# Memory and forget-gate attention heads laid as steps into the neighbouring projection chunks of a two-block transformer kernel

## The chip, the cores and the metric

The kernel runs on one core of one Trainium2 chip, as one launch. The metric is the device time of that launch in microseconds (us). Engines by their names in the profile: PE is TensorE (matmuls; PEld its weight loads), DVE is VectorE, ACT is ScalarE, POOL is GpSimd, SP is SyncE, which issues the weight transfers.

## The reference, cut to what matters

Two transformer blocks run one after the other over 256 tokens of width 1024, all in float32. The change touches only the second block, whose two layers mix tokens like this (`mk`, `mv`, `k_sh`, `v_sh` and the forget sums are computed earlier):

```
# layer 0
proj = h @ a_w_in                       # 1024 -> 3*1024 + 512
gate_b, gate_c, u, qm = split(proj)     # qm: 4 heads of 128
y_tok = gate_b * causal_depthwise_conv(gate_c * u, a_conv_w)
y_mem = softmax(qm . mk * 128**-0.5) . mv          # 4 "memory" heads
x = x + concat([y_tok, y_mem]) @ a_w_out           # 1536 -> 1024
# layer 1
q, qm = split(h @ b_w_q)                # 8 heads of 128, 4 heads of 128
y_tok = forgetting_attention(q, k_sh, v_sh, c_sh)  # 8 causal "fox" heads
y_mem = softmax(qm . mk1 * 128**-0.5) . mv1        # 4 memory heads
x = x + concat([y_tok, y_mem]) @ b_w_out           # 1536 -> 1024
```

Every head has 256 queries and 256 keys; a fox head is causal, so its first 128 queries see 128 keys.

## The kernel before, in words

**Chunks.** All weights come from memory in chunks of 1 MB (128 partitions by 2048 numbers), two buffers deep. SP loads chunk g into `W_raw` once the split of chunk g-2 is through. ACT rounds it to `W_hi` (L1012), DVE makes the rest `W_lo = W_raw - W_hi` (L1275), and PE multiplies with both parts. This split of chunk g+1 (`ahead`) is the first thing that ACT and DVE do in the body of chunk g.

**Projection chunks** (`up`, `conv`) give 256 output columns each. PE (`up_chunk`, L650 to L656) runs 16 pairs of matmuls into two of the PSUM banks 0 to 3, alternating between two pairs of banks. After the last one ACT copies one half out (`cross`, L1025), DVE adds the other (`add_halves`, L1291), DVE scales by the row factor (`by_rows`, L1300) and raises `acc_read`. **Output chunks** (`down`) take 256 rows of the weight each: 24 matmuls (`down_chunk`, L661 to L663) accumulate over all chunks into banks 4 to 7. Their input, a block of 512 columns of the stage before, is staged first: ACT rounds it (`stage_hi`, L1079, raises `st_hi`), POOL subtracts (L1809, raises `st_lo`), and `down_chunk` begins with `pe.wait_ge(st_lo, staged)`.

**The order of the work** is a list of stages written out in `make_plan`. Each engine walks the whole list in this order and runs its part of each stage; an engine never goes on to a later stage before it has issued all of its part of the earlier one. In layer 0 the list is: `conv` (12 chunks: for each group c of 4, one chunk each of gate_b, gate_c and u), `mem_q` (2 chunks), `attend memory0` (4 heads), `a_out` (6 chunks: 4 blocks of conv output, 2 of heads). In layer 1 it is `fox_q` (4 chunks), `mem_q` (2), `attend fox` (12 heads, two fox and one memory in turn), `b_out` (6).

**The convolution on POOL.** For each group c POOL waits for `acc_read` of its third chunk, multiplies gate_c by u (L1861), then makes three taps: six products (L1868), two sums (L1872), and the product with gate_b (L1873), which raises `conv_done`. Each waits for the one before.

**A head.** PE `scores` (L768), DVE `soft` (row maximum; for fox with the bias, L1338), ACT `exps` (L1086), DVE `normalise` (L1346, L1349), PE `transposes` (L786), ACT `keep_pt` (L1096), PE `values` (L803), DVE `output` (L1361). The first two or three heads' scores stand inside the last `mem_q` chunk (`open_attention`); all the rest is a block of its own, at whose start PE waits for `acc_read` of the last chunk. Scores use banks 4 to 6, transposes banks 0 and 1, values banks 2 and 3.

Of the kernel before, what the change touches and what calls it, by code (L numbers as in the profile page):

```python
# [116 lines left out]
def make_plan(w):  # L117
# [58 lines left out]
    for l in range(2):  # L176
# [30 lines left out]
def build_program(nc, a, out):  # L207
# [19 lines left out]
    with ctx:  # L227
# [163 lines left out]
        for st in stages:  # L391
            st["h0"] = h_count
            if st["kind"] == "attend":
# [7 lines left out]
                for what, h in st["what"]:  # L401
# [4 lines left out]
                    e["paired"] = st["paired"]  # L406
# [37 lines left out]
        for n, e in enumerate(heads):  # L444
# [4 lines left out]
                                (4 + 2 * (u % 2) + i,) if e["paired"] else (4 + n % 3,))  # L449
# [3 lines left out]
            e["pt_banks"] = [0, 1] if e["G"] == 3 else [i if e["paired"] else n % 2]  # L453
# [12 lines left out]
            elif e["paired"]:  # L466
                e["probs"] = region(at + (2 * (u % 2) + i) * width, width)
                e["ptile"] = [region(e["R"]["pt"] + (2 * (u % 2) + i) * 512, 512)]
                e["pt_free"] = u - 1
            else:  # L470
                e["probs"] = region(at + (n % 3) * width, width) if n % 3 < 2 else T1
                e["ptile"] = [region(e["R"]["pt"] + (n % 2) * 512, 512)]
                e["pt_free"] = u - 1
# [10 lines left out]
        k_norm = k_turn = n_glu = n_staged = n_cross = 0  # L484
        for n, st in enumerate(stages):
# [12 lines left out]
            if st["kind"] == "down":  # L498
                st["staged0"] = n_staged
                n_staged += st["n"]  # L500
                before = stages[n - 1]
                before["next_down"] = st
                st["each"] = before["kind"] == "glu" or before.get("dest") == "h"
            if st["kind"] == "attend":
                stages[n - 1]["next_attend"] = st
        before_heads = lambda st: len(stages[stages.index(st) - 1]["what"])

        def e_out_done(n):

            for st in stages:  # L510
                if st["kind"] == "attend" and st["a0"] <= n < st["a0"] + len(st["what"]):
                    return st["h0"] + n - st["a0"] + 1

# [6 lines left out]
        def down_src(st, j):  # L520
# [3 lines left out]
            return U[:, bass.ds(H0 + j * 2 * S, 2 * S)]  # L524


        opened = lambda st: {"even": 2, "dilated": 1, "memory0": 2, "fox": 3}[st["name"]]
# [17 lines left out]
        def _(sp):  # L545
# [9 lines left out]
            for st in stages:  # L555
# [41 lines left out]
                elif kind == "down":  # L597
                    ks = st["ks"]

                    def body(i):  # L600
                        for s in range(2):
                            load(g0 + 2 * i + s, slots[s],
                                 w_[:, bass.ds((2 * i + s) * ks, ks), :], ks, st["ncols"])
                    repeat(sp, n // 2, body)
# [11 lines left out]
        def _(pe):  # L616
# [15 lines left out]
            def up_chunk(g, u, slot, pair, xn=XN, first=True, between=None,  # L632
                         at=(1, 3), by_k=False):
# [66 lines left out]
            def down_chunk(st, g, staged, slot, first, final):  # L700
# [4 lines left out]
                for t in range(TT):  # L705
                    if first and t == 1 and st["src"] == "h" and not st["each"]:
# [4 lines left out]
                    for at, (ks, b) in enumerate(order):  # L711
                        if by_half and t == 0 and ks and not any(k for k, _ in order[:at]):
# [4 lines left out]
                        last = three(PS[:, 4 + 2 * t + b, 0:hi - lo],  # L717
# [73 lines left out]
            def values(u):  # L791

                both = [heads[n] for n in units[u]]
                if u >= 2:
                    pe.wait_ge(h_done, e_out_done(units[u - 2][-1]))
                for e in both:
                    d = (64 if e["paired"] else P)
                    e["o"] = PS[e["pb"]:e["pb"] + d, 2 + u % 2, 0:S]
# [16 lines left out]
                last.then_inc(s_pv, 1)  # L815

# [40 lines left out]
            for st in stages:  # L857
                g0, u0, n, kind = st["g"], st["u"], st["n"], st["kind"]
                slots, pairs = (g0 % 2, (g0 + 1) % 2), (u0 % 2, (u0 + 1) % 2)
                if kind == "norm":  # L860
                    if st["fill"] and not st["again"]:
                        fill_chunk(st, lambda: turn(st))
                    else:
                        if st["x0"] and not st["fill"]:

                            acc_free(u0)
                            for _ in range(3):
                                mm(PS[:, 2 * pairs[0], :], XN[:, 0, 0, 0:P], both_halves(XN, 0),
# [9 lines left out]
                elif kind in ("up", "glu"):  # L878
                    def body(i, ss=(0, 1)):
                        for s in ss:  # L880
# [4 lines left out]
                            if st.get("sums") and starts(i, s - 1):  # L885
# [3 lines left out]
                                     between=between, at=at, by_k=st["led"] and starts(i, s))  # L889
# [4 lines left out]
                elif kind == "conv":  # L894
                    for c in range(n):
                        up_chunk(g0 + c, u0 + c, (g0 + c) % 2, (u0 + c) % 2, first=c == 0,
                                 between=(lambda: spread(st)) if c == 1 else None, at=(1, 0))
# [53 lines left out]
                elif kind == "down":  # L951
                    for j in (0,) if n > 1 else ():
                        down_chunk(st, g0, staged + 1, g0 % 2, True, False)
# [6 lines left out]
                    def body(i):  # L960
                        for s in range(2):
                            down_chunk(st, g0 + 1 + 2 * i + s, staged + 2 + 2 * i + s,
                                       (g0 + 1 + s) % 2, False, False)
                    repeat(pe, mid // 2, body)
# [17 lines left out]
                elif kind == "attend":  # L982
                    a0, m = st["a0"], len(st["what"])

# [3 lines left out]
                    if not st["paired"]:  # L988
                        for u in us[opened(st):3]:
                            scores(u)  # L990
                    for u in us:
# [6 lines left out]
                        if not st["paired"] and u + 3 in us:  # L998
                            scores(u + 3)
# [4 lines left out]
        def _(act):  # L1004
# [76 lines left out]
            def exps(n):  # L1081
                e = heads[n]
                act.wait_ge(s_soft, n + 1)
                for t in range(TT):
# [3 lines left out]
                      accum_out=e["z"][:, t:t + 1]).then_inc(s_exp, 1)  # L1088

# [13 lines left out]
            for st in stages:  # L1103
# [39 lines left out]
                elif kind in ("up", "conv", "natural"):  # L1143
                    def body(i, ss=(0, 1)):
                        for s in ss:
# [9 lines left out]
                            if kind == "up" and s == 1 and st.get("next_attend"):  # L1155
                                exps(st["next_attend"]["a0"])
                            if kind != "natural":
                                cross(g0 + 2 * i + s, u0 + 2 * i + s, pairs[s], st.get("times", 1.0))
                    early = st.get("next_down")
                    loops = n // 2 - bool(early and n > 1)  # L1160
                    if loops and (st["led"] or st["raised"]) and kind != "conv":
# [4 lines left out]
                    else:  # L1166
                        repeat(act, loops, body)
                    if early:
# [46 lines left out]
                elif kind == "down":  # L1215
                    def body(i):
                        for s in range(2):
                            ahead(g0 + 2 * i + s, slots[s])
                            stage_hi(st, 2 * i + s + 2, g0 + 2 * i + s + 2, slots[s])
                    rounds = max(n - 2, 0) // 2  # L1220
                    repeat(act, rounds, body)
# [19 lines left out]
                elif kind == "attend":  # L1241
                    a0, m = st["a0"], len(st["what"])
# [7 lines left out]
                    lead = 2 if st["name"] in ("memory0", "fox", "even") else 1  # L1250
                    for u in st["units"]:
# [5 lines left out]
                        if u == st["units"][-1] - (2 if st["size"] == 1 else 1):  # L1257
# [4 lines left out]
        def _(dve):  # L1262
# [89 lines left out]
            def output(u):  # L1352
# [3 lines left out]
                o = PS[:, 2 + u % 2, 0:S]  # L1356
# [5 lines left out]

            def open_attention(st):


                if st["name"] == "memory0":
                    dve.wait_ge(conv_cu_done, 4)
# [50 lines left out]
            for st in stages:  # L1418
# [48 lines left out]
                elif kind == "up":  # L1467
# [4 lines left out]
                    def body(i, ss=(0, 1)):  # L1472
                        for s in ss:
# [5 lines left out]
                            if s == 1 and st.get("next_attend"):  # L1479
                                open_attention(st["next_attend"])  # L1480
# [126 lines left out]
                elif kind == "conv":  # L1607
                    for c in range(4):
                        for part in range(3):
                            j = 3 * c + part  # L1610
                            if j != 1:
                                ahead(g0 + j, (g0 + j) % 2)
# [6 lines left out]
                            if j == 0:  # L1619
                                ahead(g0 + 1, (g0 + 1) % 2)  # L1620
                                dve.wait_ge(r_kept, rows_at)
                            by_rows(dst, st["sum0"] + j + 1).then_inc(acc_read, 1)
                elif kind == "down":
# [3 lines left out]
                    repeat(dve, (n - 1) // 2, body)  # L1627
# [333 lines left out]
```

## Time and profile before

| | us |
|---|---|
| median of 3 runs (1873.0 to 1874.36) | 1873.25 |
| the profiled execution, its own time | 1875.29 |
| its span | 1873.5 |
| PE busy | 1819.4 (97%) |
| DVE busy | 1211.2 (65%) |
| ACT busy | 936.3 (50%) |
| POOL busy | 299.1 (16%) |
| chain that ended last | PE 91%, DVE 4%, ACT 3% |

Busy is the time in which an engine had an instruction running, over the span. The chain is followed back from the last instruction to whatever released each step. The layer-0 mixing stages run from about 1000 to 1129 us of the span, those of layer 1 from about 1578 to 1679 us.

### The profile page before, as it was taken

The numbers are of one execution on the slowest core, as the hardware profiler recorded it, in microseconds if no ns is written. First come the engines' busy times: TensorE is split into PE (matmuls) and PEld (weight loads), VectorE is DVE, ScalarE is ACT, GpSimd is POOL, SyncE is SP. The second block draws the span as 40 slices with busy tenths as digits, with TensorE's granted clock in tenths as the row PEclk, the third lists the DMA queues.
The fourth block names the chain that finished last, engine by engine and source line by source line (L and its number), as shares of the span: only waits on it lengthen the run. The fifth ranks groups of instructions, "written<-read, shape, count | busy, mean of one in ns | idle before, by whom it ended". The sixth has DMA issues, their size and how long they took to land.

```text
span 1873.5 us, 27530 instructions
## 1 busy us (share of the span) xinstructions
PE 1819.4 (97%) x9737; PEld 1539.3 (82%) x9737; DVE 1211.2 (65%) x1523; ACT 936.3 (50%) x1394; POOL 299.1 (16%) x255
## 2 busy tenths in 40 slices
PE   8899999999999999999999989999999999999998
PEld 6678888888877888888888878888888888778886
DVE  5866755767775665576746756674667656656664
ACT  4455545434456544464545445554554455555553
POOL 1011021211201001210022930002005021020012
PEclk9999999999999999999999999999999999999999
DMA  6326555555521665555555535555555555345553
GB/s 218 130 74 197 180 201 180 180 180 180 180 91 53 195 191 185 195 180 187 193 184 182 186 123 180 193 187 190 182 191 174 185 189 174 108 146 180 188 193 134
DMA packets 215000, 320.29 MB, mean 171 GB/s; under 512 B 6024, under 2 KB 167056, under 8 KB 214672
## 3 DMA queue, kind: packets, MB, share of 16 engines
q1 hardware_dynamic: 213616, 313.45, 50.3%
q0 software_dynamic: 1024, 5.64, 0.8%
q8 instruction: 46, 0.75, 0.2%
q10 hardware_dynamic: 288, 0.23, 0.0%
q14 instruction: 26, 0.21, 0.0%
HBM read 318.24 MB, written 1.06 MB: 170 GB/s over the span
## 4 chain that ended last, share of the span: by engine, by line
PE 91%; DVE 4%; ACT 3%; issue 1%; DMA 1%; DVEq 0%; POOL 0%; POOLq 0%; ACTq 0%; SPq 0%
PE PS L656 26%; PE PS L661 13%; PE PS L663 13%; PE PS L662 13%; PE PS L654 13%; PE PS L650 4%; PE PS L651 2%; PE PS L768 2%; DVE W_lo L1275 2%; PE PS L803 1%; PE PS L786 1%; PE PS L730 1%; ACT U L1096 1%; ACT U L1086 1%; PE PS L919 1%
## 5 line engine op out<-in xcount | busy, mean ns | idle before, releaser
L1275 DVE TENSOR_TENSOR W_lo<-W_raw,W_hi 128x1024 fp32r<-128x1024 f32 x598 | 775.5, 1336 | 292.7 <-ACT W_hi L1012 270.8
L656 PE MATMUL PS<-XN,W_hi 128*128 128x512 f32 x2072 | 740.1, 396 | 0.0
L1012 ACT ACTIVATE W_hi<-W_raw 128x1024 fp32r<-128x1024 f32 x598 | 598.6, 1050 | 176.4 <-PE PS L663 114.5
L654 PE MATMUL PS<-XN,W_lo 128*128 128x256 f32 x2072 | 579.2, 280 | 2.7 <-DVE W_lo L1275 2.7
L656 PEld LDWEIGHTS PS<-XN,W_hi 128*128 128x128 f32 x2072 | 389.6, 188 | 80.2
L654 PEld LDWEIGHTS PS<-XN,W_lo 128*128 128x128 f32 x2072 | 391.4, 189 | 16.6 <-DVE W_lo L1275 3.0
L1809 POOL TENSOR_TENSOR SX<-U,SX 128x512 fp32r<-128x512 f32 (+1 forms) x98 | 128.5, 1315 | 1141.5 <-ACT SX L1079 1141.5
L661 PE MATMUL PS<-W_hi,SX 128*128 128x512 f32 x780 | 303.9, 390 | 1.1 <-DVE W_lo L1275 1.1
L662 PE MATMUL PS<-W_lo,SX 128*128 128x512 f32 x780 | 303.0, 389 | 0.0
L663 PE MATMUL PS<-W_hi,SX 128*128 128x512 f32 x780 | 303.0, 389 | 0.0
L1025 ACT ACTIVATE T<-PS 128x512 f32<-128x512 f32 x152 | 91.0, 599 | 410.5 <-PE PS L656 410.3
L1291 DVE TENSOR_TENSOR T<-PS,T 128x512 f32<-128x512 f32 x128 | 88.4, 691 | 211.3 <-ACT T L1025 211.3
L1079 ACT ACTIVATE SX<-U 128x512 fp32r (+2 forms) x98 | 60.5, 628 | 233.5 <-PE PS L663 230.7
L661 PEld LDWEIGHTS PS<-W_hi,SX 128*128 128x128 f32 x780 | 146.4, 188 | 31.7 <-issue 1.9
L663 PEld LDWEIGHTS PS<-W_hi,SX 128*128 128x128 f32 x780 | 146.4, 188 | 30.4
L662 PEld LDWEIGHTS PS<-W_lo,SX 128*128 128x128 f32 x780 | 146.4, 188 | 30.3
L661 PE MATMUL PS<-W_hi,XN 128*128 128x512 f32 (+1 forms) x352 | 139.1, 395 | 6.0 <-DVE W_lo L1275 3.8
L663 PE MATMUL PS<-W_hi,XN 128*128 128x512 f32 (+1 forms) x352 | 137.3, 390 | 0.0
L662 PE MATMUL PS<-W_lo,XN 128*128 128x512 f32 (+1 forms) x352 | 137.2, 390 | 0.0
L650 PE MATMUL PS<-XN,W_hi 128*128 128x512 f32 x296 | 118.8, 402 | 4.5 <-DVE W_lo L1275 3.3
L661 PEld LDWEIGHTS PS<-W_hi,XN 128*128 128x128 f32 x352 | 66.6, 189 | 20.8 <-DVE W_lo L1275 5.3
L651 PE MATMUL PS<-XN,W_lo 128*128 128x256 f32 x296 | 82.2, 278 | 0.0
(166 smaller groups left out, 1532.1 us busy)
## 6 DMA issues: line engine op xcount, KB each, us to landing
W_raw<-in_ffn_w_gate_up SPq DMA_DIRECT2D x88, 1024.0 KB, 5.0
W_raw<-in_mlp_w SPq DMA_DIRECT2D x64, 1024.0 KB, 5.2
W_raw<-in_ffn_w_down SPq DMA_DIRECT2D x44, 1024.0 KB, 4.8
W_raw<-in_od_w_in SPq DMA_DIRECT2D x36, 1024.0 KB, 5.1
W_raw<-in_a_w_in SPq DMA_DIRECT2D x14, 1024.0 KB, 4.9
W_raw<-in_mem_w_kv SPq DMA_DIRECT2D x8, 1024.0 KB, 5.1
W_raw<-in_w_kvf SPq DMA_DIRECT2D x8, 1024.0 KB, 5.4
W_raw<-in_ev_w_in SPq DMA_DIRECT2D x6, 1024.0 KB, 6.3
```

The lines of the kernel that those rows point to most:

```text
L650: mm(bank, wT(W_hi, slot, k, fb), both, start=True, stop=False)
L651: mm(bank[:, S:], wT(W_lo, slot, k, fb), xn[:, k, 0, :], start=False, stop=False)
L654: mm(bank[:, S:], wT(W_lo, slot, k, fb), xn[:, k, 0, :], start=False, stop=False)
L656: last = mm(bank, wT(W_hi, slot, k, fb), both, start=False, stop=k == KD - 1)
L661: mm(bank, xh, wh, start=start, stop=False)
L662: mm(bank, xh, wl, start=False, stop=False)
L663: return mm(bank, xl, wh, start=False, stop=stop)
L1012: A(W_hi[:, slot, halves(h)], W_raw[:, slot, halves(h)], ACT.Copy).then_inc(w_hi, 1)
L1025: A(T0[:, pair, :].rearrange("p (f t) -> p f t", f=2), PS[:, 2 * pair:2 * pair + 2, S:2 * S], ACT.Copy, scale=times).then_inc(cross_out, 1)
L1275: V.tensor_tensor(W_lo[:, slot, halves(h)], W_raw[:, slot, halves(h)], W_hi[:, slot, halves(h)], ALU.subtract).then_inc(w_lo, 1)
L1291: return V.tensor_tensor(dst.rearrange("p (f t) -> p f t", f=2), PS[:, 2 * pair:2 * pair + 2, 0:S], T0[:, pair, :].rearrange("p (f t) -> p ...
L1809: nc.gpsimd.tensor_tensor(SX[:, slot, 1, 0:st["ks"] * S], down_src(st, j), SX[:, slot, 0, 0:st["ks"] * S], ALU.subtract).then_inc(st_lo, 1)
```

## The change

The blocks `attend memory0` and `attend fox` are no longer run by themselves. Each head is cut into steps: step s issues on PE `values` of head s-3, `transposes` of head s-2 and `scores` of head s, with the matching parts on DVE and ACT. `conv` chunks 0 to 6 take one step each; the `fox_q` chunks two each (steps 0 to 7), the `b_out` chunks 0 to 2 two each (8 to 13) and chunk 3 the last (14). `mem_q` now comes before `conv` and before `fox_q`. In layer 1 the four memory heads come first, then the eight fox heads, and `b_out` takes its blocks in the order 4, 5, 0, 1, 2, 3. PSUM is dealt anew: scores banks 4 and 5, transposes 6, values 7; `b_out` accumulates in banks 0 to 3. POOL's part of every stage is unchanged.

```
         if l == 0:
-            p.add("conv", "conv", 12, 12, w=w["a_w_in"])
             up("mem_q", w["a_w_in"], 3072, 2, post="copy", dest="mem_q0")
-            p.add("attend", "memory0", what=[("mem0", h) for h in range(4)])
+            p.add("conv", "conv", 12, 12, w=w["a_w_in"], steps={c: [c] for c in range(7)})
+            p.add("attend", "memory0", what=[("mem0", h) for h in range(4)], woven=True)
             down("a_out", w["a_w_out"], 1536)
         else:
-            up("fox_q", w["b_w_q"], 0, 4, post="copy", dest="fox_q")
             up("mem_q", w["b_w_q"], 1024, 2, post="copy", dest="mem_q1")
-            p.add("attend", "fox",
-                  what=[e for h in range(4) for e in (("fox", 2 * h), ("fox", 2 * h + 1), ("mem1", h))])
-            down("b_out", w["b_w_out"], 1536)
+            up("fox_q", w["b_w_q"], 0, 4, post="copy", dest="fox_q",
+               steps={c: [2 * c, 2 * c + 1] for c in range(4)})
+            p.add("attend", "fox", what=[("mem1", h) for h in range(4)] + [("fox", h) for h in range(8)],
+                  woven=True)
+            down("b_out", w["b_w_out"], 1536, order=[4, 5, 0, 1, 2, 3],
+                 steps={0: [8, 9], 1: [10, 11], 2: [12, 13], 3: [14]})
...
             e["score_banks"] = ((4 + 2 * i, 5 + 2 * i) if e["G"] == 3 else
-                                (4 + 2 * (u % 2) + i,) if e["paired"] else (4 + n % 3,))
+                                (4 + 2 * (u % 2) + i,) if e["paired"] else (4 + u % 2,))
+            e["o_bank"] = 2 + u % 2 if e["paired"] else 7
...
-            e["pt_banks"] = [0, 1] if e["G"] == 3 else [i if e["paired"] else n % 2]
+            e["pt_banks"] = [0, 1] if e["G"] == 3 else [i if e["paired"] else 6]
...
 # PE, up_chunk (steps go in at k == 3 of each half fb)
+                    if k == 3 and fb < len(woven):
+                        woven[fb]()
...
 # PE, down_chunk (steps go in after two of the four products of tile t)
-                    if first and t == 1 and st["src"] == "h" and not st["each"]:
+                    if first and st.get("weave"):
+                        if t == 0:
+                            pe.wait_ge(acc_read, st["u"])
+                    elif first and t == 1 and st["src"] == "h" and not st["each"]:
                         pe.wait_ge(h_done, st["h0"])
...
+                        if at == 2 and t < len(woven):
+                            woven[t]()
...
 # PE
+            def woven_step(st, s):
+                if s == 0:
+                    pe.wait_ge(r_kept, st["n_rows"])
+                out, turned, scored = (woven_head(st, s - back) for back in (3, 2, 0))
+                if out is not None:
+                    values(heads[out]["unit"])
+                if turned is not None:
+                    transposes(turned)
+                if scored is not None:
+                    pe.wait_ge(acc_read, heads[scored]["q_use"])
+                    scores(heads[scored]["unit"])
...
 # ACT, stage_hi
+                elif st["name"] == "a_out" and j < 4:
+                    act.wait_ge(conv_done, j + 1)
+                elif st["name"] == "b_out":
+                    act.wait_ge(h_done, st["h0"] - before_heads(st) + 2 * j + 2)
                 elif early:
-                    act.wait_ge(conv_done, 4) if st["name"] == "a_out" else act.wait_ge(
-                        h_done, st["h0"] - before_heads(st) + 8)
+                    act.wait_ge(h_done, st["h0"] - before_heads(st) + 8)
...
 # ACT, body of up, conv (down the same way, with stage_hi in the place of cross)
+                            steps = st["steps"].get(2 * i + s, ()) if "weave" in st else ()
+                            for step in steps:
+                                woven_keep(st, step)
+                                if step == steps[0]:
+                                    woven_exps(st, step)
...
                                 cross(g0 + 2 * i + s, u0 + 2 * i + s, pairs[s], st.get("times", 1.0))
+                            if len(steps) == 2:
+                                woven_exps(st, steps[1])
...
 # DVE
+            def woven_step(st, s):
+                out, scaled, scored = (woven_head(st, s - back) for back in (3, 1, 0))
+                if out is not None:
+                    output(heads[out]["unit"])
+                if scaled is not None:
+                    normalise(scaled)
+                if scored is not None:
+                    soft(scored)
...
 # DVE, conv
-                            if j != 1:
-                                ahead(g0 + j, (g0 + j) % 2)
+                            ahead(g0 + j, (g0 + j) % 2)
+                            for step in st["steps"].get(j, ()):
+                                woven_step(st, step)
...
 # POOL, down: the only line of POOL's program that differs
-                    repeat(pool, n // 2, body)
+                    repeat(pool, n // 2, body, straight="order" in st)
```

## Rows read from the trace of the kernel before

**Rows 1.** The page's slices, the granted clock of PE in 40 parts of the span.

```profile
PEclk9999999999999999999999999999999999999999
```

**Rows 2.** ACT in order of time: start, us, engine, line, operation [idle before, releaser].

```profile
1068.40 0.60 ACT L1025 ACTIVATE T<-PS 128x512 f32<-128x512 f32 x1 [3.10 <-PE PS L656]
1073.99 0.60 ACT L1025 ACTIVATE T<-PS 128x512 f32<-128x512 f32 x1 [3.10 <-PE PS L656]
...
1082.46 0.60 ACT L1025 ACTIVATE T<-PS 128x512 f32<-128x512 f32 x1 [1.93 <-PE PS L656]
1082.95 0.47 ACT L1086 ACTIVATE U<-PS,ST 128x256 f32<-128x256 f32 x1
...
1606.66 0.60 ACT L1025 ACTIVATE T<-PS 128x512 f32<-128x512 f32 x1 [3.10 <-PE PS L656]
```

**Rows 3.** PE in order of time, the end of the block of 4 heads, layer 0.

```profile
1084.71 1.77 PE L768 MATMUL PS<-U 128*128 128x256 f32 x4 [2.29 <-DVE U L1300]
...
1096.42 0.58 PE L661 MATMUL PS<-W_hi,SX 128*128 128x512 f32 x1
```

**Rows 4.** PE in order of time, inside the block of 12 heads, layer 1.

```profile
1618.44 0.87 PE L786 MATMUL PS<-K,U 128*128 128x128 f32 x3 [2.91 <-DVE U L1300]
...
1624.63 0.60 PE L786 MATMUL PS<-K,T 128*128 128x128 f32 x4
...
1626.94 0.49 PE L786 MATMUL PS<-K,U 128*128 128x128 f32 x3
...
1628.94 0.49 PE L786 MATMUL PS<-K,U 128*128 128x128 f32 x3
...
1646.13 0.58 PE L661 MATMUL PS<-W_hi,SX 128*128 128x512 f32 x1
```

**Rows 5.** PE by stretches of 1 us: stretch, length, busy (count), clock, DMA.

```profile
1085.00:1086.00 1.00, 1.00 (x4) 0.53 0.00 0
1088.00:1089.00 1.00, 1.00 (x5) 0.77 0.00 0
...
1618.00:1619.00 1.00, 0.56 (x3) 0.50 0.00 0
1623.00:1624.00 1.00, 1.00 (x3) 0.50 0.00 0
```

**Rows 6.** POOL in order of time: the last convolution group, then the first staging.

```profile
1070.78 2.14 POOL L1861 TENSOR_TENSOR U<-T 128x512 f32<-128x512 f32 x1 [0.69 <-DVE T L1300]
1073.01 6.43 POOL L1868 TENSOR_SCALAR U<-U,G 128x256 f32<-128x256 f32 x4
1079.53 1.29 POOL L1872 TENSOR_TENSOR U<-U 128x512 f32<-128x512 f32 x1
1080.92 1.82 POOL L1868 TENSOR_SCALAR U<-U,G 128x256 f32<-128x256 f32 x2
1082.83 1.27 POOL L1872 TENSOR_TENSOR U<-U 128x512 f32<-128x512 f32 x1
1084.18 1.60 POOL L1873 TENSOR_TENSOR U<-U 128x512 f32<-128x512 f32 x1
1092.40 2.49 POOL L1809 TENSOR_TENSOR SX<-U,SX 128x512 fp32r<-128x512 f32 x2 [6.62 <-ACT SX L1079]
```

**Rows 7.** DVE in order of time, after the last convolution chunk.

```profile
1069.10 0.69 DVE L1291 TENSOR_TENSOR T<-PS,T 128x512 f32<-128x512 f32 x1 [1.54 <-ACT T L1025]
1069.83 0.81 DVE L1300 TENSOR_TENSOR T<-T,RR 128x512 f32<-128x512 f32 x1
1070.56 3.44 DVE L1275 TENSOR_TENSOR W_lo<-W_raw,W_hi 128x1024 fp32r<-128x1024 f32 x2
```

**Rows 8.** DVE in order of time, the parts of one head beside other work.

```profile
1078.58 0.68 DVE L1323 TENSOR_REDUCE ST<-PS 128x2 f32<-128x512 f32 x1
...
1084.77 1.43 DVE L1349 TENSOR_SCALAR T<-T,ST 128x256 f32<-128x256 f32 x2
1090.40 0.42 DVE L1361 COPY U<-PS 128x256 f32<-128x256 f32 x1
```

More of the change, by code:

```diff
@@ L484, in build_program @@
         k_norm = k_turn = n_glu = n_staged = n_cross = 0
+        for st in stages:
+            if st["kind"] == "attend":
+                st["woven"] = st.get("woven", False)
         for n, st in enumerate(stages):
@@ L500, in build_program @@
                 n_staged += st["n"]
-                before = stages[n - 1]
+                before = stages[n - 2 if stages[n - 1].get("woven") else n - 1]
                 before["next_down"] = st
                 st["each"] = before["kind"] == "glu" or before.get("dest") == "h"
-            if st["kind"] == "attend":
+                st["bank"] = [4, 6]
+            if st["kind"] == "attend" and not st["woven"]:
                 stages[n - 1]["next_attend"] = st
-        before_heads = lambda st: len(stages[stages.index(st) - 1]["what"])
+            if st["kind"] == "attend" and st["woven"]:
+                for near in (stages[n - 1], stages[n + 1]):
+                    if near.get("steps"):
+                        near["weave"] = st
+                if stages[n + 1].get("steps"):
+                    pair = stages[n + 1]["u"] % 2
+                    stages[n + 1]["low_banks"] = [2 * pair, 2 - 2 * pair]
+        before_heads = lambda st: len(stages[stages.index(st) - 1]["what"])
+        for n, st in enumerate(stages):
+            if st.get("low_banks"):
+                st["bank"] = st["low_banks"]
+            if st["kind"] == "norm":
+                st["down_bank"] = stages[n - 1].get("bank", [4])[0] if n else 4
+            if st["kind"] == "attend" and st["woven"]:
+                use = {q["name"]: q["u"] for q in stages[:n] if q["name"] in ("mem_q", "fox_q")}
+                for what, h in st["what"]:
+                    e = next(e for e in heads if e["st"] is st and (e["bias"] == "fox", e["h"]) == (what == "fox", h))
+                    e["q_use"] = use["fox_q" if what == "fox" else "mem_q"] + h // 2 + 1
         def e_out_done(n):
@@ L698, in fill_chunk, with down_chunk @@
                 last.then_inc(chunk_done, 1)
-            def down_chunk(st, g, staged, slot, first, final):
+            def down_chunk(st, g, staged, slot, first, final, woven=()):
                 pe.wait_ge(st_lo, staged)
@@ L888, in body @@
                                      first=s == 0 and (starts(i) or not st["raised"]),
-                                     between=between, at=at, by_k=st["led"] and starts(i, s))
+                                     between=between, at=at, by_k=st["led"] and starts(i, s),
+                                     woven=woven_steps(st, 2 * i + s) if "weave" in st else ())
                     if n > 1:
@@ L981, in _ @@
                         turn_heads(R["mla_kn"], 2 * pairs[b] - 2 * b, range(4 * b, 4 * b + 4))
-                elif kind == "attend":
-                    a0, m = st["a0"], len(st["what"])
+                elif kind == "attend" and not st["woven"]:
                     pe.wait_ge(acc_read, u0)
                     us = st["units"]
-                    if not st["paired"]:
-                        for u in us[opened(st):3]:
-                            scores(u)
                     for u in us:
@@ L1166, in _ @@
                     else:
-                        repeat(act, loops, body)
-                    if early:
+                        repeat(act, loops, body, straight="weave" in st)
+                    if early and st["name"] != "fox_q":
                         stage_early(early)
@@ L1240, in _ @@
                     stage_early(st["next_down"])
-                elif kind == "attend":
-                    a0, m = st["a0"], len(st["what"])
+                elif kind == "attend" and not st["woven"]:
+                    a0 = st["a0"]
                     if stages[stages.index(st) - 1]["kind"] != "up":
@@ L1699, in _ @@
                     V.scalar_tensor_tensor(f_abs, f_z, -1.0, f_z, ALU.mult, ALU.max).then_inc(f_v, 1)
-                elif kind == "attend":
-                    a0, m = st["a0"], len(st["what"])
+                elif kind == "attend" and not st["woven"]:
                     us = st["units"]
```

105 lines of the change are left out of this document (62 added, 43 removed).

## The prediction

> **What bounds the kernel now.** First the page: PE is busy 97% of the span, and its chain holds 91% of what ended last; the slices of its clock are all nines [rows 1]. So a change counts only by what it does to PE: matmul time, idle time, or time at the lower clock. Then ACT's order of time around the two blocks of heads: each half copied out by `cross` marks the end of a projection chunk, and 1068.40 to 1073.99 gives the period of an undisturbed chunk, 5.59 us [rows 2]. That is the clock by which I count. Third, PE's own order of time, for where the output projection starts [rows 3, 4], and PE's clock by stretches [rows 5].
>
> Layer 0: the first `mem_q` chunk ended at 1073.99 [rows 2]; with nothing between, `a_out` could have begun one chunk later, at 1079.58. It began at 1096.42 [rows 3]. The four heads cost 16.8 us. Layer 1: the first `mem_q` chunk ended at 1606.66 [rows 2], so `b_out` could have begun at 1612.25; it began at 1646.13 [rows 4]. The twelve heads cost 33.9 us.
>
> What of this is PE's own work? In the middle of the layer-1 block PE never waits, and the starts of successive `transposes` give a full head: 2.31 us for a memory head (1624.63 to 1626.94), 2.00 us for a fox head (1626.94 to 1628.94) [rows 4]. So the work is 4 x 2.31 = 9.2 us in layer 0 and 8 x 2.00 + 4 x 2.31 = 25.2 us in layer 1. The rest, 7.6 and 8.7 us, is idle time at the start (2.29 and 2.91 us, waiting for the last chunk's `by_rows` [rows 3, 4]) and at the end, and the clock: after these idle stretches PE ran at half clock (1.2 of 2.4 GHz), about 3.4 us of it in layer 0 (granted 0.53 in 1085 to 1086, back in 1088 to 1089 at 0.77) and nearly 6 us in layer 1 [rows 5]. These 16.3 us are all that laying the heads into the chunks can win.
>
> **Part 1, the steps in the chunks.** PE issues the same matmuls. A step adds a switch into the projection's matmuls and back; the nearest row is the first output matmul after the heads, 0.58 us [rows 3] against the page's mean of 0.39 for its line, so 0 to 0.2 us a step; I take the middle, 0.1. Layer 0 has 7 steps: 9.2 + 0.7 = 9.9 us (9.2 to 10.6). Layer 1 has 15: 25.2 + 1.5 = 26.7 us (25.2 to 28.2).
>
> Do the steps wait? What is queued behind a waiting step on PE is the whole projection, so this matters. Steps lie 8 pairs of matmuls apart in layer 1 (half of 5.59, 2.8 us, plus the step, about 5.0), a whole chunk apart in layer 0 (about 8.0). Every part of a head has one step's distance to its successor. DVE per memory head: maximum 0.68, two products 0.6 to 1.43, output 0.42 [rows 8], some 0.35 of small ones: 2.1 to 2.9 us. In layer 1 a chunk of 10.2 us holds a split of 2.7 (two halves at the page's mean of 1.34), add and scale of 1.4 and two heads, some 8.5 us. I walked through it in order: the split is over 5.3 us after a chunk's start; the second step on PE comes at 6.15, its `values` need an output ready at 5.7 and its `transposes` (7.1) a product ready at 6.5. The smallest slack is 0.4 us; I put no wait. ACT fits in the same gaps. With SP nothing changes but the order of blocks; the loads have 8 to 10 us a chunk in place of 5.6, and POOL has no part in heads. Moving `mem_q` ahead of `conv` puts the wait for the row factor ahead of the next split, as `fox_q` has it now in layer 1: there the chunks ran on. I put 0.
>
> **Part 2, the start of `b_out`.** It accumulates in banks that the projections used and waits for `acc_read` of the last `fox_q` chunk: copy, add, scale. The same wait is the 2.29 us before the heads of layer 0; from the copy's start (1082.46 [rows 2]) to PE's start (1084.71 [rows 3]) it is 2.25 us. It stays, only moved. The first input block is staged before it, since its heads were done two chunks earlier. Both times that such a gap occurred the clock halved [rows 5]: 3.4 us at half clock does the work of 1.7, so 1.7 is lost (0 to 3.0; I take the case of layer 0, the same length of gap). Layer 1: 26.7 + 2.25 + 1.7 = 30.7 us against 33.9: 3.2 us won (from 6.6 won to 0.2 lost).
>
> **Part 3, the start of `a_out`, where I see the change fail.** Before, two `mem_q` chunks and four heads lay between the last convolution chunk and `a_out`, 1068.40 to 1096.42. Under them POOL finished the last group: it started 1070.78 and ended 1085.78 [rows 6], 17.4 us after the chunk, and nobody waited. Now `a_out` follows that chunk directly. ACT may stage blocks 0 and 1 early, as their `conv_done` is long there. But `st_lo` is POOL's, and POOL's program still has the whole `conv` stage ahead of `a_out`: the subtraction for block 0 is queued behind the last group's last product, and PE's first `a_out` matmul behind the subtraction. From the copy of the last chunk:
>
> - to POOL's start 2.38 us (1068.40 to 1070.78), behind DVE's add and scale [rows 7]; the product gate_c x u, with its gap, to 4.61 (1073.01) [rows 6];
> - six products of the taps. Four took 6.43 us while DVE was splitting, two took 1.82 while it was idle [rows 6]. Now DVE has one split, 3.44 us from 1070.56, that is until 5.6 us after the copy [rows 7], then none, because the next chunk's buffer is only freed by PE. So one slow, 1.6, and five at 0.91: 6.15;
> - two sums, 1.29 and 1.27, the last product at 1.3 (1.60 was beside DVE's work), gaps of 0.09 x 5: 4.3 [rows 6]. The group ends at 15.1;
> - the subtraction 1.25 (2.49 for two) and 0.1 to be seen, PE's start 0.1: 16.6 us.
>
> If everything ran at the slow rates it would be 17.4 + 1.4 = 18.8; if all products were fast, 15.9. I take 16.6, since DVE's idleness is certain. PE is idle as long, and starts `a_out` at half clock: 1.7 to 3.0 us lost, I take 2.0. What was hidden before is now in the open.
>
> The Trainium skill (SBUF — State Buffer, Who interferes with whom) says that a DVE instruction with two SBUF inputs and a GpSimd instruction that reads SBUF exclude each other for a whole instruction. By it the products fall to the fast rate once the split is through, sum 16.6; by the slow rows as they stand it would be 18.8. The two rates in the rows above agree with the rule.
>
> Layer 0: 9.9 + 16.6 + 2.0 = 28.5 us against 16.8: 11.7 us lost (10.1 to 15.6, the low end 9.2 + 15.9 + 1.7).
>
> **The sum.** 11.7 - 3.2 = 8.5 us slower. On the profiled execution (1875.29, of which the span is 1873.5) that is 1883.8; on the median of 1873.25, 2.0 lower for the same kernel, 1881.8. Ends: +3.5 and +15.8, that is 1877 to 1889.
>
> **The rivals.**
>
> *The subtraction does not wait (faster).* If POOL's part of `a_out` were not held by the last group, `a_out` would start after its first matmuls' own needs. PE's wait would be at most the 2.25 of part 2, the clock 1.7: layer 0 is 9.9 + 2.25 + 1.7 = 13.9, 2.9 won, and with layer 1 6.1 won: 1867.1. For it: ACT's waits were relaxed block by block just so. Against it: in the rows POOL runs one instruction after the other, its `SX` rows after the group's [rows 6], and one stage list orders it. 8%. The Trainium skill (TensorE: Matmul & The Clock Gate, Architectural detail: the array is 16× 32×32, not 1× 128×128) calls GpSimd's queue strict first in, first out, and lets only TensorE pull weight loads ahead; by it this rival is out. No row shows the two ready at once, so its chance stays.
>
> *DVE and ACT become the bound in the woven convolution chunks (slower still).* There the maximum, `exps` and the copy follow in one ring: add 0.7, scale 0.8, split up to 3.44 beside POOL, output 0.42, products 1.43, maximum 0.68 and small ones 0.35, exps 1.0 (two of 0.47), copy 0.6: 9.4 us against PE's 8.0 [rows 2, 7, 8]. Five such chunks lose 7.0, less the 3 us by which the split is early: 4 us, 1886. It decides from a ring of about 8.6 us on. For it: POOL works during these chunks. Against it: a split takes 2.7 at the page's mean, products 0.6 where POOL is idle, and the ring is then 8.0 or less. 14%.
>
> *No clock loss and cheaper steps.* The forecast's own low end, not a case apart.
>
> **How the numbers follow.** Forecast 78%, the free subtraction 8%, the ring 14%. The median of this kernel is known to about 0.2% (3.75 us), so "same" is 1869.5 to 1877.0. Faster: the first rival, 8%. Same: the forecast's low tail, 7%. Slower: 85%. The range of 8 in 10 leaves out the free subtraction, and the tails: 1875 to 1889.
>
> **What would show it right or wrong.** (1) PE before the first `a_out` matmul (L661's kind): idle some 16.5 us, released by POOL's `SX` row; none or 2 us there breaks part 3. (2) POOL's last group: 15 us from the last copy, with five of six products near 0.91. (3) Woven chunks: the copies 8.0 us apart in `conv` chunks 2 to 4 and 10 in `fox_q`, and no PE waits at L803 or L786; periods of 9 and more mean the ring. (4) `b_out` starts 2.3 us after the last copy, at half clock for some 3.4 us. (5) Over all, mixing in layer 1 is 3 us shorter, in layer 0 nearly 12 longer. I am wrong in the whole if layer 0 is not longer.

## The result, and the profile after

| | before | after |
|---|---|---|
| median of 8 runs each, us | 1873.12 (1871.45 to 1874.78) | 1878.58 (1876.11 to 1880.44) |
| ratio to before, 95% interval | | 1.0028 (1.0019 to 1.0037) |
| profiled execution, its own time | 1875.29 | 1878.81 |
| its span | 1873.5 | 1877.0 |
| PE busy | 1819.4 | 1817.7 |

The change makes the kernel 0.28% slower, 5.5 us. To see where, I need a stretch that begins and ends at the same events in every kernel. I take the time from the start of ACT's copy of the row factor (`RR`, in the layer's second projection chunk) to the start of its first square of the new `x` after the output projection. Before, layer 0 takes 117.57 us by that measure (1009.67 to 1127.24) and layer 1 89.89 (1587.09 to 1676.98). The kernel after beside it:

```
            before   after    difference
layer 0     117.57   129.93   +12.4
layer 1      89.89    82.19    -7.7
```

The rest of the span differs by about 1 us, less than runs differ among themselves. The two layers pull against each other, which the total alone does not tell.

The waits of PE at the steps and at the two output projections of the kernel after (engine, tile, line, what released it: us in total, times, longest):

```profile
PE PS L697 <- POOL SX L1897: 17.6, 1, 17.6
PE PS L697 <- DVE U L1386: 2.3, 1, 2.3
PE PS L845 <- DVE U L1447: 0.3, 1, 0.3
PE PS L827 <- DVE U L1435: 0.2, 1, 0.2
```

The first is the start of `a_out`, the second the start of `b_out`; the last two are the only waits in a step, one in layer 1 and one in layer 0. The next two fences are ACT and PE in order of time around the last convolution chunk of the kernel after; 1086.65 answers to 1068.40 in [rows 2], and 1104.24 to 1096.42 in [rows 3].

```profile
1010.43 0.60 ACT L1080 ACTIVATE T<-PS 128x512 f32<-128x512 f32 x1 [2.40 <-PE PS L692]
...
1075.95 1.14 ACT L1137 ACTIVATE SX<-U 128x512 fp32r<-128x512 f32 x2
...
1086.65 0.60 ACT L1080 ACTIVATE T<-PS 128x512 f32<-128x512 f32 x1 [3.10 <-PE PS L692]
1087.14 1.99 ACT L1067 ACTIVATE W_hi<-W_raw 128x1024 fp32r<-128x1024 f32 x2
1112.66 0.63 ACT L1137 ACTIVATE SX<-U 128x512 fp32r<-128x512 f32 x1 [23.52 <-PE PS L699]
```

```profile
1104.24 0.80 PE L697 MATMUL PS<-W_hi,SX 128*128 128x512 f32 x1 [17.63 <-POOL SX L1897]
```

From 1010.43 to 1086.65 lie twelve chunks, 12 x 5.59 = 67.1, so the four heads cost 9.1 us in them. Then PE does nothing for 17.6 us. The data were not what it waited for: ACT had staged its part of the first two blocks at 1075.95, before the last chunk ended, and only POOL's part was missing. The first `a_out` chunk ran to 1112.66, when ACT was let go, 8.4 us where it took 6.0 before (1096.42 to ACT's next staging at 1102.43). The reason is the clock, which was granted at half until past 1109. PE by stretches of 1 us (stretch, length, busy and count, clock, DMA):

```profile
1089.00:1090.00 1.00, 0.00 (x0) 0.67 1.01 414
...
1104.00:1105.00 1.00, 0.76 (x2) 0.50 0.00 0
1109.00:1110.00 1.00, 1.00 (x4) 0.59 0.00 0
1110.00:1111.00 1.00, 1.00 (x6) 1.00 0.00 0
```

What POOL did meanwhile, in order of time, to be laid beside [rows 6]:

```profile
1087.87 1.27 POOL L1961 TENSOR_TENSOR U<-U 128x512 f32<-128x512 f32 x1
1089.83 2.11 POOL L1949 TENSOR_TENSOR U<-T 128x512 f32<-128x512 f32 x1 [0.69 <-DVE T L1386]
1092.04 4.58 POOL L1956 TENSOR_SCALAR U<-U,G 128x256 f32<-128x256 f32 x4
1096.71 1.26 POOL L1960 TENSOR_TENSOR U<-U 128x512 f32<-128x512 f32 x1
1098.07 1.82 POOL L1956 TENSOR_SCALAR U<-U,G 128x256 f32<-128x256 f32 x2
1099.97 1.26 POOL L1960 TENSOR_TENSOR U<-U 128x512 f32<-128x512 f32 x1
1101.31 1.26 POOL L1961 TENSOR_TENSOR U<-U 128x512 f32<-128x512 f32 x1
1102.93 1.26 POOL L1897 TENSOR_TENSOR SX<-U,SX 128x512 fp32r<-128x512 f32 x1 [0.36 <-POOL U L1961]
```

POOL is busy almost from end to end. The first row is still the last product of the third group, beside DVE's scale of the last chunk:

```profile
1088.07 1.61 DVE L1386 TENSOR_TENSOR T<-T,RR 128x512 f32<-128x512 f32 x1
```

The scale took 0.81 in [rows 7]. So the last group begins 3.2 us after the copy (89.83 less 86.65), not 2.4.

Now PE in layer 1 of the kernel after: one whole step of memory heads in the middle of a `fox_q` chunk, then one of fox heads in a `b_out` chunk (values, transposes, scores, back to the projection). They are to be laid beside the starts in [rows 4]:

```profile
1613.38 1.03 PE L845 MATMUL PS<-U 128*128 128x256 f32 x4
1614.25 0.60 PE L827 MATMUL PS<-K,U 128*128 128x128 f32 x4
1614.68 1.03 PE L809 MATMUL PS<-U 128*128 128x256 f32 x4
1615.36 0.47 PE L690 MATMUL PS<-XN,W_lo 128*128 128x256 f32 x1
...
1650.16 0.82 PE L845 MATMUL PS<-U 128*128 128x256 f32 x4
1650.82 0.49 PE L827 MATMUL PS<-K,U 128*128 128x128 f32 x3
1651.14 0.82 PE L809 MATMUL PS<-U 128*128 128x128 f32 x4
1651.62 0.58 PE L697 MATMUL PS<-W_hi,SX 128*128 128x512 f32 x1
```

A memory step takes 1.98 us from start to start (1613.38 to 1615.36), a fox step 1.46 (1650.16 to 1651.62), and some 0.2 more for the slow first matmul behind it. In the block of the kernel before they had 2.31 and 2.00, at the same full clock.

### The profile page after: what moved, and what is told of

Read it like the earlier page. It is cut to its first block, busy times and chain, and to the rows that moved or that the text cites. A ratio compares the mean times of both kernels' runs of the same rounds, so it can differ in the third digit from the quotient of the medians.

```text
span 1877.0 us, 27450 instructions
## 1 busy us (share of the span) xinstructions
PE 1817.7 (97%) x9737; PEld 1540.5 (82%) x9737; DVE 1210.5 (64%) x1523; ACT 935.5 (50%) x1394; POOL 294.6 (16%) x255
## 4 chain that ended last, share of the span: by engine, by line
PE 89%; DVE 5%; ACT 3%; DMA 1%; issue 1%; POOL 1%; DVEq 0%; POOLq 0%; ACTq 0%; SPq 0%
PE PS L692 25%; PE PS L697 13%; PE PS L699 13%; PE PS L698 13%; PE PS L690 12%; PE PS L686 4%; DVE W_lo L1361 2%; PE PS L687 2%; PE PS L809 2%; PE PS L845 1%; PE PS L827 1%; PE PS L771 1%; ACT U L1144 1%; ACT U L1164 1%; PE PS L980 1%
## 5 line engine op out<-in xcount | busy, mean ns | idle before, releaser
L697 PE MATMUL PS<-W_hi,SX 128*128 128x512 f32 x780 | 306.8, 393 | 21.6 <-POOL SX L1897 17.6
```

What stands on the lines that cost most here:

```text
L697: mm(bank, xh, wh, start=start, stop=False)
```

## The experiments

My theory: layer 0 loses by the order of POOL's instructions alone, layer 1 wins by what the block had wasted, and the two are independent. The rivals: the steps themselves cost time in the convolution chunks; `a_out` needs the convolution's data or POOL's pace, whatever the order. "Local" is the stretch defined above. Ratios are to the kernel before, timed on the same chip.

| kernel | median us | before there | ratio (95%) | layer 0 local | layer 1 local |
|---|---|---|---|---|---|
| l1_only | 1865.23 | 1873.87 | 0.9955 (0.9943 to 0.9968) | 117.53 | 82.20 |
| l0_only | 1887.23 | 1873.87 | 1.0067 (1.0054 to 1.0080) | 129.72 | 89.92 |
| sub_first | 1872.72 | 1873.87 | 0.9989 (0.9980 to 0.9997) | 122.66 | 82.24 |
| sub_between | 1868.70 | 1873.87 | 0.9966 (0.9953 to 0.9979) | 118.55 | 80.58 |
| sub_early | 1866.19 | 1875.30 | 0.9953 (0.9939 to 0.9966) | 115.11 | 82.24 |
| best | 1861.28 | 1875.30 | 0.9929 (0.9916 to 0.9943) | 115.05 | 78.78 |
| warm_pe | 1874.72 | 1875.30 | 0.9995 (0.9985 to 1.0005) | 128.20 | 80.58 |
| block_shift | 1868.58 | 1875.30 | 0.9965 (0.9951 to 0.9978) | 115.16 | 85.26 |
| dve_sub | 1856.32 | 1874.50 | 0.9899 (0.9884 to 0.9914) | 110.46 | 78.83 |
| l1_relax | 1863.42 | 1874.50 | 0.9940 (0.9926 to 0.9954) | 117.51 | 78.83 |

**One layer at a time.** l1_only has the stages of layer 0, and all that belongs to them, as before the change; l0_only the same for layer 1.

```
-            up("mem_q", ...); p.add("conv", ..., steps={c: [c] for c in range(7)})
-            p.add("attend", "memory0", ..., woven=True)
+            p.add("conv", ...); up("mem_q", ...)
+            p.add("attend", "memory0", ...)
```

> Layer 1 as in the changed kernel (twelve heads as steps), layer 0 as before (its four heads a block after mem_q). Theory: the two layers are independent, the changed kernel lost 12.3 us in layer 0 and won 7.8 in layer 1, so this kernel is 7.8 us faster than the kernel before: 1865.3 against 1873.1. Rival (my forecast's own sizes, the rest of the traces' difference being noise): 3.2 us faster, 1869.9. Rival (the steps in the projection chunks are what loses time): not faster than before.

> Layer 0 as in the changed kernel, layer 1 as before. Theory: 12.3 us slower than the kernel before, 1885.4, with one PE wait of about 17.6 us for POOL's subtraction. My forecast's size for it: 11.7 slower. Rival (the layers are not additive, the loss belongs to both): 5 to 6 us slower.

8.6 us faster and 13.4 slower. The local stretches agree with those of the changed kernel and the kernel before to 0.3 us in either layer, so the layers are independent, and the changed kernel is their sum. The forecast's 3.2 us for layer 1 is refuted (the interval of l1_only is 6.0 to 10.7 us). What inside layer 1 wins is read from traces: the steps, the order of the heads and the PSUM banks changed together, and no run takes them apart.

**The order of POOL's subtractions.** sub_first lets `a_out` take the blocks of the memory heads first, and POOL subtracts for these two ahead of its last group (ACT's waits follow the new order, and the two subtractions are gone from their old place):

```
+            down("a_out", w["a_w_out"], 1536, order=[4, 5, 0, 1, 2, 3])
...
                     for c in range(4):
+                        if c == 3:
+                            lo_early(0); lo_early(1)      # POOL: L1809's subtraction for a_out
                         pool.wait_ge(acc_read, st["u"] + 3 * c + 3)
```

sub_between adds `if c == 3 and tap: lo_early(4 - tap)` after each of the first two taps.

> The changed kernel, with a_out's blocks in the order 4, 5, 0, 1, 2, 3 (memory heads first) and POOL's subtractions for the first two issued ahead of the last convolution group. No work is added or taken. Theory (the order of POOL's instructions makes the stall): a_out begins as soon as the last convolution chunk ends, its third chunk waits for the group to end and one subtraction, 10.9 us later at 17.4: idle 6.5, and 1.7 at half clock, against 17.6 and 2.4 before: 11.8 us faster than the changed kernel, 1866.8. Rival (a_out needs the convolution's data, or POOL's pace is the limit): the wait stays near 17 us, 1878.6. Rival (the loss comes from the steps in the convolution chunks, by the ring of DVE and ACT): 1876 or more.

> As sub_first, and the subtractions for the third and fourth a_out chunk are put between the taps of the last convolution group. Theory: nothing of a_out waits for POOL by more than 1 us; 20 us faster than the changed kernel, 1858.6, which is 14.5 faster than the kernel before. Rival (order of POOL irrelevant): 1878.6. Rival (POOL too slow with two subtractions more in the group, the last block late): 3 to 6 us less gain, 1862 to 1865, with a wait at the last chunk of a_out.

No instruction was added, and layer 0 became 7.3 and 11.4 us shorter. That refutes both rivals as the whole cause: a different order takes most of the wait away, with every step still in its chunk. That the data were not missing is shown by ACT's staging at 1075.95, not by this run, in which the order of the blocks changed too. But I had expected 11.8 and 20. The waits of PE in layer 0 of sub_first, and POOL there:

```profile
PE PS L697 <- POOL SX L1903: 4.7, 1, 4.7
PE PS L697 <- POOL SX L1951: 4.2, 1, 4.2
```

```profile
1088.89 1.27 POOL L1978 TENSOR_TENSOR U<-U 128x512 f32<-128x512 f32 x1
1090.24 3.81 POOL L1951 TENSOR_TENSOR SX<-U,SX 128x512 fp32r<-128x512 f32 x2
```

The last copy was at 1087.67. POOL was then still finishing the third group, and the two "early" subtractions came after it, at 1090.24, beside DVE's split, at 1.9 us each in place of 1.25. I had taken POOL to be waiting there.

**Earlier still, and the start of b_out.** sub_early is sub_between with the first two subtractions moved ahead of POOL's third group (`if c == 2`) and ACT's staging of those blocks behind conv chunk 7. best adds this:

```
-                        if t == 0:
-                            pe.wait_ge(acc_read, st["u"])
+                        pe.wait_ge(acc_read, st["u"] - 1 + t)
```

and stages `b_out`'s first block ahead of the last `fox_q` chunk's steps.

> As sub_between, but ACT stages the first two a_out blocks (both of memory heads, ready since conv chunk 6) after conv chunk 7 and POOL subtracts them ahead of its third convolution group. In sub_between POOL was still at that third group when PE finished the last conv chunk, so PE idled 4.2 us, ran its first a_out chunk at half clock (8.6 us instead of 5.4) and waited 2.0 for the last. Theory (order and lag of POOL make all of it): these 9 us go, 1859.5, that is 9.2 faster than sub_between. Rival (POOL's total work binds: what is taken at the start comes back as a wait at the last a_out chunks): 3 to 5 us faster than sub_between, 1864 to 1866, with a POOL wait there of 4 us or more.

> sub_early, and in layer 1 b_out's first tile waits only for the last but one fox_q chunk (its banks are that chunk's), the second tile for the last; ACT stages b_out's first block ahead of the last chunk's steps. Theory: PE's wait of 2.3 us at the start of b_out goes, and with it the half clock behind it (1.8 us): 4 us faster than sub_early, 1855.5, which is 18 faster than the kernel before. Rival (a new wait of the same length, for POOL's subtraction, takes its place): 0 to 1 faster than sub_early.

Of the 9 us, sub_early won 3.4 in layer 0, and the whole kernel only some 2.4, since its layer 1 had the half clock that sub_between's had not (82.24 and 80.58). The rival on POOL's amount of work was nearer in size, though its wait of 4 us at the end is only 2.3:

```profile
PE PS L697 <- POOL SX L1906: 2.3, 1, 2.3
PE PS L697 <- POOL SX L1954: 0.4, 1, 0.4
PE PS L690 <- DVE W_lo L1368: 0.3, 1, 0.3
```

POOL and then DVE of sub_early, at the same time:

```profile
1092.31 2.15 POOL L1969 TENSOR_TENSOR U<-T 128x512 f32<-128x512 f32 x1
1094.56 4.28 POOL L1976 TENSOR_SCALAR U<-U,G 128x256 f32<-128x256 f32 x2
```

```profile
1091.01 4.53 DVE L1368 TENSOR_TENSOR W_lo<-W_raw,W_hi 128x1024 fp32r<-128x1024 f32 x2
```

DVE's split takes 4.53 us here; where POOL has nothing to do (1137.12 in the same trace) it takes 2.36. POOL's four products take 4.28, where two took 1.82 above (3.64 for four). Each engine holds up the other, and PE, which in the kernel before never waited for either in `a_out`, now waits for both. best over sub_early is 3.5 us shorter in layer 1 (4 expected), and PE's wait for DVE at the start of `b_out` is gone from its rows.

**The subtractions on DVE.** dve_sub is best with this in DVE's `down` and `conv` bodies, and the same lines gone from POOL's:

```
+                            if j >= 10:                        # in conv: the first two blocks
+                                lo_dve(st["next_down"], j - 10)
...
+                            if st["name"] == "a_out":          # in down: the other four
+                                lo_dve(st, 2 * i + s + 2)
```

l1_relax is layer 0 as before the change with layer 1 of best.

> As best, but DVE instead of POOL makes the six subtractions of a_out (the first two at the end of conv chunks 10 and 11, the others one chunk ahead). In best POOL's subtractions lie inside its last convolution group, and POOL and DVE slow each other: splits of 4.5 us instead of 2.4, a_out chunks of 6.1 us instead of 5.4, a wait of 2.3 at the last one. Theory (POOL's own amount of work is what is left of layer 0's loss): layer 0 runs without a PE wait, 7.7 us shorter than before the change and 5 shorter than in best, where it is 2.5 shorter: 0.990 of the kernel before, 1855.5 on 1873.9. Rival (DVE is now late with its splits, since each subtraction waits in front of the next split): no gain over best, 0.993.

> Layer 0 as before the change, layer 1 as in best (steps, and the relaxed start of b_out). Theory (the layers are independent): 11.2 us faster than the kernel before, 0.994. With dve_sub it tells what the steps in layer 0 are worth when nothing waits for POOL: 7 to 8 us. Rival (they are worth nothing there): the same time as dve_sub.

Both came out as the theory had them. The waits of PE in layer 0 of dve_sub, all of them:

```profile
PE PS L826 <- DVE U L1441: 0.7, 1, 0.7
```

Layer 0 is 110.46 us, 7.1 shorter than with the block, of the 7.6 that the trace had offered. So my theory that the order alone was at fault holds for most of it only: from 129.93 us the order took layer 0 to some 115, and the last 4.6 us went only when DVE took over the six subtractions. dve_sub beats both kernels: 1.0% faster than before, 18 us.

**The clock in the open wait.** warm_pe keeps PE at work during the wait, results thrown away:

```
+                if first and st["name"] == "a_out":
+                    pe.wait_ge(h_done, st["h0"])
+                    for _ in range(74):
+                        mm(PS[:, 7, :], XN[:, 0, 0, 0:P], both_halves(XN, 0), start=True, stop=True)
```

> The changed kernel with 74 idle matmuls on PE (their results are thrown away) between the last conv chunk and a_out, about 16.8 us of matmuls inside the 17.6 us wait. Theory: POOL ends when it did, a_out starts when it did, but at full clock: the first a_out chunk takes 5.5 to 6 us instead of 8.4, the kernel is 2.4 us faster than the changed one, 1876.2. Rival (the slow first chunk is not the clock): 1878.6.

```profile
1105.24 0.50 PE L697 MATMUL PS<-W_hi,SX 128*128 128x512 f32 x1 [1.03 <-POOL SX L1901]
...
1111.07 0.63 ACT L1141 ACTIVATE SX<-U 128x512 fp32r<-128x512 f32 x1 [21.11 <-PE PS L699]
```

(The second row is ACT's, let go by the chunk's end.) The first chunk took 5.8 us in place of 8.4, with the granted clock at 1.00 from 1104 on; POOL was no sooner. So the slow first chunk was the clock. Layer 0 as a whole is only 1.7 us shorter, because its convolution chunks took 0.7 longer and POOL 0.2. The kernel's 0.9995 is better than 1.0028 by some 6 us, more than was expected: layer 1 is 1.6 us shorter too, without having been changed, and the other half of the difference is not accounted for (the two intervals allow 2.6 to 9.7). In layer 1 PE waited the same 2.30 us before `b_out`, and this time the clock stayed, first row; in the kernel after it fell, second row:

```profile
1638.00:1639.00 1.00, 1.00 (x7) 1.00 0.07 16
```

```profile
1639.00:1640.00 1.00, 1.00 (x4) 0.50 0.00 0
```

**What a head costs PE.** block_shift is the kernel before, with values one head later:

```
                         if not st["paired"] and u + 3 in us:
                             scores(u + 3)
-                        values(u)
+                        values(u - 1)          # and values(u) after the last
```

> The kernel before, with one thing changed: in the two blocks of heads PE issues the values of a head one head later (transposes u, scores u+3, values u-1). Theory: in the block each head's PE period of 2.00 and 2.31 us held a wait of 0.3 to 0.45 us for ACT's copy of the transposes, which the trace does not show as idle, since in the woven kernel the same instructions take 1.65 and 1.97 us. With the values later this wait goes, and DVE, which has 1.8 us a head, is next: 2 to 4 us faster than the kernel before, 1871. Rival (the block's period was PE's own work, as my forecast had it): no change, 1873.9.

6.7 us faster, more than expected: 2.4 in layer 0 and 4.6 in layer 1. First the kernel before, one fox head of [rows 4] with ACT's copy of its transposes:

```profile
1627.27 0.82 PE L768 MATMUL PS<-U 128*128 128x128 f32 x4
1628.21 0.89 PE L803 MATMUL PS<-U 128*128 128x256 f32 x4
```

```profile
1627.47 0.60 ACT L1096 ACTIVATE U<-PS 128x512 f32<-128x512 f32 x1 [0.74 <-PE PS L786]
```

The copy ends at 1628.07, and `values` starts 0.14 us later; it is so in the heads around this one too (1630.07 and 1630.21). Now PE in the block of block_shift, one fox head and the memory head after it:

```profile
1625.40 0.55 PE L786 MATMUL PS<-K,U 128*128 128x128 f32 x3
1625.79 0.82 PE L768 MATMUL PS<-U 128*128 128x128 f32 x4
1626.45 0.82 PE L803 MATMUL PS<-U 128*128 128x256 f32 x4
1627.28 0.66 PE L786 MATMUL PS<-K,T 128*128 128x128 f32 x4
...
1629.29 0.49 PE L786 MATMUL PS<-K,U 128*128 128x128 f32 x3
```

Periods of 1.88 and 2.01 us where they had been 2.00 and 2.31. So the period in the block was not PE's own work, though the trace shows no idle time in it. This makes some 2.0 us over the twelve heads. It is not all: in the kernel after the same work takes 1.46 and 1.98 us, so block_shift's heads wait still, and no run shows for what. Another 1.2 came from the block's end: from the third-last `transposes` to `b_out` it took 6.57 us before (1639.56 to 1646.13, with PE waits of 0.78, 1.22 and 0.78 for ACT's copies) and 5.37 now. The last 1.4 or so is the clock. Before, PE worked at half clock from 1618.4 to about 1624.4, 5.9 us; here from 1617.4 to the middle of the second row, 3.1 us, and half of the difference is lost work:

```profile
1618.00:1619.00 1.00, 1.00 (x6) 0.50 0.00 0
1620.00:1621.00 1.00, 1.00 (x6) 0.76 0.00 0
1621.00:1622.00 1.00, 1.00 (x10) 1.00 0.00 0
```

So of the 6.7 us only the first two parts, and what belongs to them in layer 0, are owed to the edit.

## Why the prediction was right, and where it was not

The forecast was 8.5 us slower; measured were 5.5 (3.6 to 6.9 by the interval), inside the range and with the sign given 85%. The range held with luck in it: layer 1's 7.7 us won lie outside the 6.6 that I had as its best, while layer 0 came 0.7 worse than its sum.

- *Part 3, the start of `a_out`.* Right in mechanism and place. Terms: heads 9.9, wait 16.6, clock 2.0, sum 28.5; measured 9.1, 17.6, 2.4, sum 29.1. The wait was 1.0 short, 0.8 of it because I began POOL's group at [rows 6]'s 2.38 us after the copy. POOL's third group, under the last three chunks, where no steps are, took 17.0 us (1072.13 to 1089.14) where it had taken 16.1 (1054.00 to 1070.09), and beside its end DVE's scale took twice its time. Why the third group was slower no run shows. The lag is the same in sub_first. The fast rate for the products held: four in 4.58 with one slow one, two in 1.82. The Trainium skill (SBUF — State Buffer, Who interferes with whom) has it that a DVE instruction with two SBUF inputs and a GpSimd instruction that reads SBUF shut each other out for a whole instruction; the trace of sub_early agrees, where DVE's split took 4.53 us beside POOL and 2.36 without it.
- *Part 1, the steps in layer 1.* The term that was mis-sized. I read 2.00 and 2.31 us a head as PE's work, and added 0.1 for each step: 26.7 us. With the wait at `b_out` and the clock at my sizes, layer 1's measured 7.7 won leaves 22.2, 4.5 less. The error is in the sentence "in the middle of the layer-1 block PE never waits". It waited for ACT's copy of the transposes in every head. Between the starts of `scores` and `values` lay 0.94 us in the block, fox or memory; in a step the next matmul starts 0.48 us after a fox head's `scores` (1651.14 to 1651.62) and 0.68 after a memory head's (1614.68 to 1615.36). The rows of the four matmuls last 0.82 and 1.03 us all the same, and so cover all or most of such a wait. block_shift bears out that there was a wait; it won back about 2 of the 5.6 us by which the periods differ (8 x 0.54 and 4 x 0.33).
- *What the change could win at most.* I wrote that 16.3 us were all. That leaned on the same reading of PE's work: dve_sub is 18.2 us faster, 7.1 of it in layer 0 and 11.1 in layer 1, where I had 7.6 and 8.7.
- *No step waits.* Right: the rows hold 0.3 us in all the steps of layer 1 and 0.2 in those of layer 0.
- *Part 2.* The 2.30 us came as forecast (2.25), and 1.7 for the clock in the profiled execution; sub_between and warm_pe, where the clock stayed, show that the second does not come in every execution.
- *The rivals.* A subtraction that does not wait did not come about, and dve_sub shows what it would have been worth: 7.1 us in layer 0, where I had 2.9. The ring of DVE and ACT shows in one pair of copies: 1031.14 to 1039.85 is 8.7 us. It never reached PE, whose next chunk was copied out 5.0 us later. My sign of 8.0 us apart in `conv` chunks 2 to 4 was wrong (6.8, 8.7 and 5.0): with four heads only step 3 holds all three parts of a head.

## What to carry to other kernels

When work is moved out from between two stages, list what ran under it on the other engines, and look for an in-order queue whose later part the next stage needs: here two `mem_q` chunks and four heads had covered 17 us of POOL. Measure each changed place between two events common to both kernels; +12.4 and -7.7 hid in a total of +5.5. The better half of such a change can be had alone (0.9955); with the queue relieved and the start of `b_out` relaxed as well it came to 0.9899.

## What the runs showed of the hardware that I had not expected

A period without idle time in PE's rows is no proof that PE is the bound there: nearly 0.5 us of waiting in 2.00 us did not show. Compare the spacing of starts of the same instructions in two surroundings.

The same 2.30 us gap in PE's work was followed by half clock in one execution (0.50 in 1639 to 1640) and by full clock in another (1.00 in 1638 to 1639), with 1.6 us between their layer-1 stretches. The profiled executions of l1_only, sub_first and sub_early fell to 0.50 behind that gap as well, and sub_between, which has no added matmuls, did not. Stretches of 82.2 and 80.6 us for the same code in the table above are these two.
